# Six 576 KB moving sums of the first MLP matrix: from GpSimd arithmetic to ScalarE bases and adding transfers

## The reference, cut to what matters

```
h = _layer_norm(ALPHA * h + (mix @ w_out + b_out), ln1_g, ln1_b)
f = jnp.square(jax.nn.relu(h @ w_mlp1 + b_mlp1)) @ w_mlp2 + b_mlp2
h = _layer_norm(ALPHA * h + f, ln2_g, ln2_b)
```

## Time and profile before

| | before |
|---|---|
| median of 3 runs | 805.94 us (802.87 to 806.76) |
| the profiled execution | 806.29 us |
| its span on the core | 804.6 us |
| PE busy | 779.3 us (97%) |
| DVE busy | 524.5 us (65%) |
| ACT busy | 426.6 us (53%) |
| POOL busy | 170.8 us (21%) |
| DMA | 90.57 MB, 113 GB/s on average |

### The profile page before, as it was taken

One profiled execution on the slowest core, in us unless ns is written; L12 is line 12 of the kernel. 1 busy time (PEld: TensorE's weight loads), 2 busy tenths in 40 slices (PEclk: granted clock), 3 DMA queues, 4 the chain that ended last, 5 costly groups with the idle time before them and its releaser, 6 DMA issues.

```text
span 804.6 us, 14048 instructions
## 1 busy us (share of the span) xinstructions
PE 779.3 (97%) x5720; PEld 751.9 (93%) x5720; DVE 524.5 (65%) x749; ACT 426.6 (53%) x666; POOL 170.8 (21%) x207
## 2 busy tenths in 40 slices
PE   8999999999999999999999789999999999998995
PEld 6999899998989999999999789999999999998994
DVE  5823444754647377876879677878875886665644
ACT  5633345654645575562554375488336763376324
POOL 2100000572120110016625800000000000000356
PEclk9999999999999999999999899999999999999998
DMA  8632131112111121243201356656657547644103
GB/s 303 265 124 97 53 113 53 54 56 80 53 54 56 49 79 54 79 133 109 99 3 53 85 147 166 178 135 182 175 153 185 142 138 186 177 116 144 56 2 117
DMA packets 27070, 90.57 MB, mean 113 GB/s; under 512 B 2864, under 2 KB 7104, under 8 KB 26624
## 3 DMA queue, kind: packets, MB, share of 16 engines
q1 hardware_dynamic: 22592, 74.26, 26.8%
q0 software_dynamic: 4000, 15.10, 10.1%
q10 hardware_dynamic: 416, 0.33, 0.1%
HBM read 84.84 MB, written 4.85 MB: 111 GB/s over the span
## 4 chain that ended last, share of the span: by engine, by line
PE 76%; ACT 7%; DVE 6%; DMA 4%; issue 3%; POOL 3%; SPq 0%; DVEq 0%; ACTq 0%; POOLq 0%
PE lin L750 7%; PE lin L751 7%; PE lin L752 7%; PE z L1267 6%; PE z L1268 6%; PE z L1269 6%; DMA raw<-w_sets 4%; PE z L1006 3%; PE lin L1144 2%; PE lin L1145 2%; PE lin L1146 2%; PE lin L1284 2%; PE lin L1286 2%; PE lin L1285 2%; PE lin L1267 2%
## 5 line engine op out<-in xcount | busy, mean ns | idle before, releaser
L750 PE MATMUL lin<-h_hi,whi 128*128 128x288 f32 (+1 forms) x448 | 135.1, 301 | 5.2 <-DVE wlo L2096 5.2
L751 PE MATMUL lin<-h_lo,whi 128*128 128x288 f32 (+1 forms) x448 | 133.5, 298 | 0.0
L752 PE MATMUL lin<-h_hi,wlo 128*128 128x288 f32 (+1 forms) x448 | 132.9, 297 | 0.0
L750 PEld LDWEIGHTS lin<-h_hi,whi 128*128 128x128 f32 x448 | 85.2, 190 | 6.7 <-DVE wlo L2096 5.4
L751 PEld LDWEIGHTS lin<-h_lo,whi 128*128 128x128 f32 x448 | 85.3, 190 | 0.1
L752 PEld LDWEIGHTS lin<-h_hi,wlo 128*128 128x128 f32 x448 | 85.3, 190 | 0.0
L1838 ACT ACTIVATE whi<-raw 128x1024 fp32r<-128x1024 f32 x48 | 50.7, 1056 | 44.1 <-PE z L1269 21.7
L2693 DVE TENSOR_TENSOR wlo<-raw,whi 128x1024 fp32r<-128x1024 f32 x48 | 58.6, 1221 | 19.4 <-ACT whi L1838 19.4
L2096 DVE TENSOR_TENSOR wlo<-raw,whi 128x1024 fp32r<-128x1024 f32 x41 | 51.1, 1246 | 28.5 <-ACT whi L1360 26.6
L1360 ACT ACTIVATE whi<-raw 128x1024 fp32r<-128x1024 f32 x38 | 40.0, 1053 | 50.6 <-PE lin L752 32.6
L1267 PE MATMUL z<-f_ops,whi 128*128 128x288 f32 x176 | 53.1, 301 | 3.8 <-DVE wlo L2693 2.6
(11 more groups left out here) (458 smaller groups left out, 2605.7 us busy)
## 6 DMA issues: line engine op xcount, KB each, us to landing
raw<-w_stream SPq DMA_DIRECT2D x64, 512.0 KB, 3.2
raw<-w_sets SPq DMA_DIRECT2D x48, 512.0 KB, 3.9
raw<-w_sets POOLq DMA_DIRECT2D x24, 512.0 KB, 6.8
w_fifth<-w_sets SPq DMA_DIRECT2D x12, 512.0 KB, 5.3
r<-x_t SPq DMA_DIRECT2D x8, 296.0 KB, 5.0
kcache<-k_cache SPq DMA_DIRECT2D x1, 2048.0 KB, 10.1
vcache<-v_cache SPq DMA_DIRECT2D x1, 2048.0 KB, 8.0
y<-r SPq DMA_DIRECT2D x8, 160.0 KB, 1.8
```

What stands on the lines that cost most here:

```text
L750: pe.matmul(out, w_h, hi, start=first, stop=False)
L751: pe.matmul(out, w_h, lo, start=False, stop=False)
L752: return pe.matmul(out, w_l, hi, start=False, stop=last)
```

## The change

POOL's arithmetic on `hs_sums` goes. ACT writes the first, negated term of each sum (`hs_base`): T3 in four instructions of 288 columns with the bias difference, V4 in one of 1152 columns, both behind `tile(4, 1)`; V5 in one, V6 in four with a bias, behind `tile(5, 1)`. POOL adds the other terms with six accumulating transfers from SBUF to SBUF of 576 KB each: T3 and V4 after the first bases, V5 and V6 after the second ones; then it waits until these four have landed (`hs_in` 64) and issues the second add of V6 and that of V4 (the finished V5 sum). Behind these six, as before behind the arithmetic, come the accumulating transfers of the sets. `residual2` and `hs_round` wait for all six (`hs_in` 96). On DVE `x_sum(t + 1)` moves from the front of s = 6 to its end, in all sets. `split_end(0)` moves from behind the last set to the front of its s = 6, on ACT ahead of block C12, on DVE ahead of `last_lo` C22. No matmul is added or taken away.

```diff
@@ ACT
             def hs_round(o):
-                act.wait_ge(hs_made, 13)
+                act.wait_ge(hs_in, 16 * HS_ADDS)
@@
             def residual2(m):
-                act.wait_ge(hs_made, 13)
+                act.wait_ge(hs_in, 16 * HS_ADDS)
@@
+            def hs_base(o):
+                def put(x, r, shift):
+                    nc.scalar.activation(x, r, ACT.Identity, bias=shift, scale=-1.0).then_inc(hs_based, 1)
+                if o in (V5, V4):
+                    blocks = r1[:, 0:PRS, half(1)] if o == V5 else r1[:, PRS:KC, half(0)]
+                    nc.scalar.activation(hs_sums[:, o - V5, :, :], blocks, ACT.Copy, scale=-1.0).then_inc(hs_based, 1)
+                else:
+                    for k in range(PRS):
+                        put(hs_sums[:, o - V5, k, :], r1[:, k, half(1)],
+                            bias_diff[:, k:k + 1] if o == T3 else vec(V_LN1_B + PRS + k))
@@
                 tile(u, 0)
                 tile(u, 1)
+                if u == 4:
+                    act.wait_ge(ones_2_made, 3)
+                    hs_base(T3)
+                    hs_base(V4)
+                elif u == 5:
+                    act.wait_ge(f_lo_done, 11)
+                    hs_base(V5)
+                    hs_base(V6)
@@
+                    if t == N_SETS - 1 and s == 6:
+                        split_end(0)
                     if kind == "in" and s == 6:
                         block_relu(t, C12)
@@
-            split_end(0)
             set_tail(N_SETS - 1, 0)
@@ DVE
-                    if s == 6:
-                        x_sum(t + 1)
-                        if inner and p < 3:
-                            v_sum(t, V5)
-                            v_sum(t, T3)
+                    if s == 6 and inner and p < 3:
+                        v_sum(t, V5)
+                        v_sum(t, T3)
...
                     if inner and s == 6:
+                        if t == N_SETS - 1:
+                            split_end(0)
                         if p == 3:
                             last_lo(t, C22)
                         else:
                             v_sum(t, V6)
+                    if s == 6:
+                        x_sum(t + 1)
@@
-            split_end(0)
             last_lo(N_SETS - 1, C12)
@@ POOL
-            def hs_shift(o, k, shift):
-                x = hs_sums[:, o - V5, k, :]
-                nc.gpsimd.tensor_scalar(x, x, shift, 0.0, ALU.add, ALU.add).then_inc(hs_made, 1)
-            pool.wait_ge(n1_scaled, 2 * KC)
-            pool.wait_ge(f_lo_done, 11)
-            nc.gpsimd.tensor_tensor(hs_sums[:, V5 - V5, :, :], r1[:, 0:PRS, half(0)], r1[:, 0:PRS, half(1)],
-                                    ALU.subtract).then_inc(hs_made, 1)
...
+            def hs_add(o, block):
+                pool.dma_start(hs_sums[:, o - V5, :, :], block, accum_op=ALU.add).then_inc(hs_in, 16)
+            pool.wait_ge(hs_based, SET_IN + HS_T3V4)
+            hs_add(T3, r1[:, PRS:KC, half(1)])
+            hs_add(V4, r1[:, PRS:KC, half(1)])
+            pool.wait_ge(hs_based, SET_IN + HS_T3V4 + HS_V5V6)
+            hs_add(V5, r1[:, 0:PRS, half(0)])
+            hs_add(V6, r1[:, PRS:KC, half(1)])
+            pool.wait_ge(hs_in, 16 * 4)
+            hs_add(V6, r1[:, 0:PRS, half(0)])
+            hs_add(V4, hs_sums[:, 0, :, :])
```

More of the change, by code:

```diff
@@ L352, in encoder_step @@
         SET_IN = 16
+        HS_ADDS, HS_T3V4, HS_V5V6 = 6, 1 + PRS, 1 + PRS
         unit_in = [sem(f"unit_in{s}") for s in range(RAW)]
@@ L391, in encoder_step @@
         al_in, de_in, ga_in, si_base = x_in[0]
-        ap_base = x_in[1][0]
+        ap_base, hs_based = x_in[1][:2]
         si_in, ap_in = sem("si_in"), sem("ap_in")
@@ L398, in encoder_step @@
             sem("first_copied"), sem("z_summed"), sem("relu_done"), sem("plain_done"), sem("v_made"))
-        hs_made, hs_hi_done, hs_lo_done = sem("hs_made"), sem("hs_hi_done"), sem("hs_lo_done")
+        hs_in, hs_hi_done, hs_lo_done = sem("hs_in"), sem("hs_hi_done"), sem("hs_lo_done")
         t_made, ones_2_made = sem("t_made"), sem("ones_2_made")
@@ L3171, in _ @@
             nc.gpsimd.tensor_tensor(bias_diff[:, :], vecs[:, V_LN1_B + PRS:V_LN1_B + KC],
-                                    vecs[:, V_LN1_B:V_LN1_B + PRS], ALU.subtract).then_inc(hs_made, 1)
-            def hs_shift(o, k, shift):
-                x = hs_sums[:, o - V5, k, :]
-                nc.gpsimd.tensor_scalar(x, x, shift, 0.0, ALU.add, ALU.add).then_inc(hs_made, 1)
-            pool.wait_ge(n1_scaled, 2 * KC)
-            pool.wait_ge(f_lo_done, 11)
-            nc.gpsimd.tensor_tensor(hs_sums[:, V5 - V5, :, :], r1[:, 0:PRS, half(0)], r1[:, 0:PRS, half(1)],
-                                    ALU.subtract).then_inc(hs_made, 1)
[L3182 to L3195, removed]
+                                    vecs[:, V_LN1_B:V_LN1_B + PRS], ALU.subtract).then_inc(ones_2_made, 1)
+            def hs_add(o, block):
[9 more added lines that the diff above has]
+            hs_add(V4, hs_sums[:, 0, :, :])
             for t in range(N_SETS):
```

## The result

Timed in turns on one chip, the changed kernel takes 815.68 us (median of 4, 813.47 to 818.37) against 804.97 (median of 4, 802.87 to 806.76): ratio 1.0132, 95% interval 1.0096 to 1.0168, that is +10.6 us (7.7 to 13.5). It is slower, as forecast, by more than twice the forecast +4.4. The profiled execution took 815.82 us, 9.5 more than that of before, with a span of 814.1.

The account below looks back on a forecast made before the run. TensorE, busy 97%, was taken to bound the kernel, with set 0 hanging on SI's landing. Terms 8.3 - 1.65 + 0.25 - 2.5 = +4.4 us gave 810.7 against the profiled 806.29, median 810.3; range 801 to 815.5.

Parts of the forecast that it names:

- What bounds set 0: Set 0: the change's worth there is read off SI's landing alone, with the chain behind it unchanged.
- L: Time at which set 0's SI lands: forecast to move from 462.8 to 471.1, 8.3 us later.
- TensorE's path: Rival in set 0: TensorE's own path is the bound, total -11.6 us, some 794; chance 0.02.
- Cost of an add: Six adding transfers ahead of set 0's SI: 3.8 us of the engines for small pieces, 3.4 for whole rows.
- the rivals on the rate: Engine time per add: plain 1.6 us (0.16), two reads 2.9 (0.10), bytes alone 3.4 (0.22), small pieces 4.8 (0.15).
- the plain rate: Rival on set 0's adds: 1.6 us each, SI landing at 460.6, total -6.1 us, 799.8; chance 0.16.
- The half clock in set 0: Set 0: half clock moves from third to second block product, winning 1.65 us; other bound nothing won.
- `split_end(0)`: End unit: wait of 2.3 us shrinks to 0.1, new 1.2 at chunk 5; gain 2.5 us, bounds 0.9 and 2.5.
- `x_sum`: Starts of sets 4 and 8: `x_sum` behind costs 0.25 us at set 4, nothing at 8; bounds 0 and +0.6.
- the dear rate: Rival on set 0's adds: small pieces cost three times, 4.8 us each, total +9.4 us, 815.3; chance 0.15.

Follow-up runs that it names:

- e_sifirst: Kernel before, with GpSimd issuing the accumulating transfer of set 0's SI ahead of its arithmetic on the moving sums: 802.81 us, ratio 0.9958.
- e_adds_plain: As e_adds, but the six transfers copy instead of adding (sums wrong): 805.21 us, ratio 0.9992 against the kernel before.
- e_adds: Kernel before with the moving sums alone changed (ScalarE's bases, six adding transfers); `x_sum` and `split_end(0)` stay: 814.01 us, ratio 1.0122.
- e_split: Kernel before with `split_end(0)` alone moved ahead of block C12: 804.59 us, ratio 0.9975.
- e_xmid: Kernel before with `x_sum(t + 1)` moved only behind `v_sum` V5 and T3, ahead of the rest of the step: 806.34 us, ratio 1.0001.
- e_adds_rows: As e_adds, but each add reads whole 4608 B rows instead of 1152 B pieces (sums of other blocks): 811.80 us, ratio 1.0074 against the kernel before.
- e_xsum: Kernel before with `x_sum(t + 1)` alone moved behind the weight and square sums of s = 6: 809.79 us, ratio 1.0051.
- e_xsum_in: Kernel before with `x_sum(t + 1)` moved behind all of s = 6 in sets 2 and 6 alone: 807.93 us, ratio 1.0027.
- e_adds_sifirst: As e_adds, but GpSimd issues set 0's SI ahead of the six adding transfers: 807.65 us, ratio 1.0026 against the kernel before.

## Why the prediction was right in sign and wrong in size

- **What bounds set 0: right.** The bound was L, SI's landing, and not TensorE's path. e_sifirst moves L the other way and the time follows (-3.4 us); e_adds_plain brings L forward by 8.6 us against e_adds and is 9 to 10 us shorter than it.
- **Cost of an add: right.** Taken 3.8 us, measured 3.8 in the changed kernel and 3.7 in e_adds. V5 and V6 landed at 458.5 on before's axis (forecast 458.7) and SI at 470.8 (forecast 471.1). All the rivals on the rate fall, from both sides: the plain rate is that of copies (1.6), and whole rows would have made it 3.1. That the size fits so well has luck in it: 3.8 was made of 3.4 for the bytes times 1.12 for small pieces, and the runs show 3.1 and 1.2.
- **The half clock in set 0: right.** It falls on the second block product now, which takes 5.3 us (473.93 to the end at 479.2) and is over before the first copy at 479.55. Set 0 costs 6.42 by the ledger; forecast 8.3 - 1.65 = 6.65. The 1.65 isn't certain, though: in e_split and e_xmid set 0's waits of 2.2 and 2.4 us at the same place are followed by the full clock.
- **`split_end(0)`: right.** -2.0 (interval -3.3 to -0.7) alone, -2.3 by the ledger, forecast -2.5. The waits are 0.3 and 1.0, forecast 0.1 and 1.2; the clock stays at its upper level. Of the 2.3, 1.5 are the half clock behind the old wait, and only four of the nine traces that keep this wait show it; where the clock stays up, the move is worth 0.8.
- **`x_sum`: this step failed.** The forecast put it at 0.25 us, bounds 0 and +0.6, with the words "X comes 2 to 3 us later, but is wanted one block product (3.2 us) behind SI". It measured +4.1 us alone (2.6 to 5.6). In the ledger of the changed kernel its own share is some 3.0: 2.65 in sets 3 and 7, for which the forecast had nothing, and 0.2 at each of sets 4 and 8. Two things are wrong in that sentence. X comes 5.2 us later, because it is moved past a wait of 2.02 us and not only past the instructions. And I asked when TensorE wants X, not who waits for X first: that is ScalarE, in whose list the first copy stands behind X's high part. At sets 4 and 8, where the forecast looked, its reading holds: the five instructions ahead of `set_lo(V5)` take no longer in the new order. In it ScalarE's high part of SI comes first, then the rest; after, at set 4:

```profile
564.10 1.06 ACT L1839 ACTIVATE whi<-raw 128x1024 fp32r<-128x1024 f32 x1 [0.94 <-DMA raw<-w_sets]
```

```profile
565.19 1.23 DVE L2716 TENSOR_TENSOR wlo<-raw,whi 128x1024 fp32r<-128x1024 f32 x1 [0.58 <-ACT whi L1839]
...
568.14 0.75 DVE L2785 TENSOR_TENSOR f_ops<-f_plain,f_ops 128x576 fp32r<-128x576 f32 x1
```

  `set_lo(V5)` starts 4.04 us behind SI's landing, before 4.28 (554.82 to 559.10). VectorE's idle time, 0.58 here and 1.14 at set 8, is SI's landing passed on by ScalarE.
- **What no step could hold.** 0.8 us of the profiled difference arises in the first 8 us of the kernel, 0.6 without a wait, and 1.1 because SI lands later at sets 4 and 8. Together: 4.4 forecast, + 2.7 for `x_sum`, + 0.2 at the end unit, - 0.2 in set 0, + 0.8 + 0.6 + 1.1, make 9.6; the two profiled executions differ by 9.5. Between the medians it is +10.6. So `x_sum` is the step that failed, and nearly half of the gap between +4.4 and the measured time is in it; the rest is in terms that one trace can't tell from chance.
- **The range.** Its upper end of 815.5 was made from the dear rate alone. The bounds of `x_sum` were taken from TensorE's wants and not from the lists of the two engines between; with an upper bound of 4 us there it would have held the time. The median, 815.68, lies just above it.

## What to carry to other kernels

An accumulating transfer takes a queue's time as an instruction takes an engine's: here six adds of 3.8 us each put a weight load 8 us later that stood behind them, while the engine that issued them was idle; putting the urgent load first recovered most of it, and then the adds were late, because loads ran beside them. When a step is moved back in one engine's list, go to the engine that waits for its result first and read what stands behind that wait in its list; the consumer at the end of the chain may want the result much later and still be held up by something else. And work that makes another engine stand costs wherever it is put: moving it moves the stall.

## What the runs showed of the hardware that I had not expected

- An adding transfer of 576 KB within SBUF takes 3.7 us of 16 engines in pieces of 1152 B and 3.1 in whole rows; a copy in pieces of 1152 B takes 1.6. The issue of a small-piece add keeps GpSimd for some 1.3 us (two in 2.70), that of a whole-row add 0.86 (e_adds_rows), that of a load of 512 KB 0.87 (e_sifirst).
- The same wait of TensorE before the end unit, 2.33 us in nine kernels that leave `split_end(0)` in place, is followed by the half clock in four profiles (before, e_sifirst, e_adds_rows, e_adds_plain: granted 0.50 to 0.63 in the first us) and by the full clock in five (e_adds, e_xsum, e_xmid, e_xsum_in, e_adds_sifirst). That is a term of 1.6 us which one profile can't give for sure.
- TensorE's waits for V5's low part at sets 4 and 8 differ between kernels that have the same code there: 1.09 and 1.28 us before, 2.10 and 1.76 in e_split, 0.93 and 1.59 in e_sifirst, 1.81 and 1.58 in e_adds. They follow SI's landing (the table above). Why the same 512 KB land after 7.0 us in one trace and 9.3 in another stays open; it limits how well one trace can tell a cost below 1 us.
